# A two-block transformer on one core: router matmuls split into halves, expert gates moved into the first expert step, norms by halves, masks written singly, parameter loads moved

## The reference

```python
x = x + ((g_gla * y_gla + g_att * y_att) @ w_out[l])
x = x + hier_moe(rms_norm(x, norm2_g[l]), ...)   # 32 experts: group by argmax, then the top 2 of its 8
...
for i in range(2):                               # second block
    z = rms_norm_2(h, g_mix[i]) @ w_in[i]
    h = h + concatenate([y_a, y_b, y_c]) @ w_out[i]
    hn = rms_norm_2(h, g_ffn[i])
    h = h + (swiglu(hn, ...) if i == 0 else moe_swiglu(hn, ...))   # 8 experts, top 2
    h = h + (p[i] @ ple_proj_w[i]) * sigmoid(rms_norm_2(h, g_ple[i]) @ ple_gate_w[i])
return rms_norm_2(h, g_final)
```

## Time and profile before

| | |
|---|---|
| median of 3 runs | 2471.05 us (2470.52 to 2474.22) |
| profiled execution | 2472.59 us, of which the span of the trace is 2470.8 us |
| PE busy | 2319.1 us, 94% |
| DVE busy | 1842.4 us, 75% |
| ACT busy | 1467.2 us, 59% |
| POOL busy | 49.6 us, 2% |
| granted TensorE clock, mean | 0.971 |

### The profile page before, as it was taken

The page is one execution under the profiler, slowest core; times in us unless marked ns, Lnnn a source line. Parts: engine busy times, 40 slices in busy tenths (PEclk is TensorE's granted clock), DMA queues, the critical chain, the costliest instruction groups (busy, mean ns, idle before and its releaser), DMA issues.

```text
span 2470.8 us, 30555 instructions
## 1 busy us (share of the span) xinstructions
PE 2319.1 (94%) x12418; PEld 1891.6 (77%) x12418; DVE 1842.4 (75%) x1894; ACT 1467.2 (59%) x1400; POOL 49.6 (2%) x47
## 2 busy tenths in 40 slices
PE   7999987999999997988999998879999999999996
PEld 6878766888888885776788777668888888888885
DVE  5885658888898985776554577578888978888884
ACT  5354536776777774534443553466776767767764
POOL 0000000000000000020000002000000000000000
PEclk9999998999999998999999999989999999999999
DMA  9444445999999997406464551249999989999990
GB/s 231 128 124 136 153 145 186 363 367 358 366 359 367 357 368 231 138 3 196 138 203 171 166 163 50 81 177 363 356 366 357 358 300 349 358 368 355 366 344 34
DMA packets 281227, 617.64 MB, mean 250 GB/s; under 512 B 31848, under 2 KB 130408, under 8 KB 243696
## 3 DMA queue, kind: packets, MB, share of 16 engines
q1 hardware_dynamic: 279664, 611.33, 71.4%
q10 hardware_dynamic: 1408, 4.19, 0.5%
HBM read 612.34 MB, written 1.05 MB: 248 GB/s over the span
## 4 chain that ended last, share of the span: by engine, by line
PE 86%; DVE 7%; ACT 4%; issue 2%; POOL 0%; DMA 0%; DVEq 0%; ACTq 0%; SPq 0%
PE ps L566 25%; PE ps L567 25%; PE ps L568 25%; DVE ring_parts L590 2%; PE ps L2745 2%; PE ps L2098 1%; ACT high_parts L586 1%; PE ps L3023 1%; PE ps L667 1%; DVE arena L3280 0%; DVE arena L1325 0%; PE ps L3036 0%; PE ps L2068 0%; PE ps L2109 0%; PE ps L2110 0%
## 5 line engine op out<-in xcount | busy, mean ns | idle before, releaser
L590 DVE TENSOR_TENSOR ring_parts<-ring,high_parts 128x2048 fp32r<-128x2048 f32 (+1 forms) x574 | 1283.4, 2276 | 181.6 <-ACT high_parts L586 170.0
L586 ACT CAST high_parts<-ring 128x2048 fp32r<-128x2048 f32 (+1 forms) x574 | 1079.5, 1897 | 203.9 <-PE ps L568 190.6
L568 PE MATMUL ps<-high_parts,arena_parts 128*128 128x512 f32 (+2 forms) x1560 | 620.2, 398 | 0.0
L566 PE MATMUL ps<-high_parts,hT_parts 128*128 128x512 f32 (+2 forms) x1120 | 456.4, 408 | 30.5 <-DVE ring_parts L590 12.6
L567 PE MATMUL ps<-ring_parts,hT_parts 128*128 128x512 f32 (+2 forms) x1120 | 445.3, 398 | 0.0
L566 PE MATMUL ps<-high_parts 128*128 128x512 f32 x912 | 365.2, 400 | 0.0
L567 PE MATMUL ps<-ring_parts,high_parts 128*128 128x512 f32 x912 | 359.3, 394 | 0.0
L568 PE MATMUL ps<-high_parts 128*128 128x512 f32 x912 | 356.5, 391 | 0.0
L568 PEld LDWEIGHTS ps<-high_parts,arena_parts 128*128 128x128 f32 x1560 | 299.5, 192 | 68.9
L566 PE MATMUL ps<-high_parts,arena_parts 128*128 128x512 f32 x744 | 293.8, 395 | 3.2 <-DVE arena_parts L2273 2.3
L567 PE MATMUL ps<-ring_parts,arena_parts 128*128 128x512 f32 x744 | 292.9, 394 | 0.0
(11 more groups left out here) (525 smaller groups left out, 1831.0 us busy)
## 6 DMA issues: line engine op xcount, KB each, us to landing
ring<-in_moe_w SPq DMA_DIRECT2D x248, 1024.0 KB, 5.4
ring<-in_w_gate SPq DMA_DIRECT2D x64, 1024.0 KB, 5.3
ring<-in_w_up SPq DMA_DIRECT2D x64, 1024.0 KB, 5.2
ring<-in_w_down SPq DMA_DIRECT2D x64, 1024.0 KB, 5.3
ring<-in_w_in SPq DMA_DIRECT2D x104, 256.0 KB, 4.5
ring<-in_ffn_w SPq DMA_DIRECT2D x44, 512.0 KB, 4.8
ring<-in_w_in SPq DMA_DIRECT2D x20, 1024.0 KB, 5.0
ring<-in_moe_w SPq DMA_DIRECT2D x32, 512.0 KB, 4.8
```

The costliest lines, as they stand in the source:

```text
L566: pe.matmul(dst, a_hi, b_hi, start=first, stop=False, skip_group_check=True)
L568: return pe.matmul(dst, a_lo, b_hi, start=False, stop=last, skip_group_check=True)
L586: act.copy(high_flat(p), raw_flat(p)).then_inc(upper, 1)
L590: dve.tensor_tensor(raw_flat(p, ring_parts_flat), raw_flat(p), f32(high_flat(p)), ALU.subtract).then_inc(split, 1)
```

## The change

- **Routers.** The router matmuls of half of x stand inside the last projection; x·gain is made in halves before rstd is known; ACT multiplies it by rstd into the high rows, DVE (not POOL) makes the low rows; the slots of the tokens come right behind "routed", and two barriers between the stages are gone.
- **Gates.** The gates are made on DVE and ACT behind the first four splits of the first expert step. PE's `gates(b)` stands behind the last up piece of a step, not behind up 1, and waits for a new signal; this holds in each bucket or group that has one, so in the second group of `moe2` too.
- **Norms.** One half of the squares is made with the first half of x, and the table of Sqrt (in the feed-forward that of Silu too) is asked for by a small instruction ahead of the need. DVE adds the halves.
- **Feed-forward.** The split of the first down piece is moved ahead of the stage.
- **Masks.** POOL signals each of the two masks by itself; the wait for a mask ends earlier; the last LT mask is left out; POOL's copy comes behind the first pair. DVE makes TT before T.
- **Low-rank slots.** 9 becomes 10, and 12 becomes 13.
- **Parameter loads.** For layer 0 they stand behind four pieces of `in_0`, not six, and wait for the transposes of x, not for the last expert's matmuls.

```diff
@@ out_1 (and out_1_2), PE and DVE
+                if slot == 2 * (n_ab + 15):
+                    router_half_pe(pe, moe1, 0)
...
+                    if slot == 7 and l:
+                        router_half_pe(pe, moe2, 0)
...
+                    moe_gained_dve(dve, moe1, 0)
...
+        def norm_half_act(act, half):
+            for t in range(NT):
+                cols = slice(half * 512, (half + 1) * 512)
+                ins = act.activation(nt_sq[:, t * 512:(t + 1) * 512], x[:, t, cols], ACT.Square, accum_out=half_sums[half][:, t:t + 1])
+            if half:
+                ins.then_inc(sig("norm_sq"), 1)
+            else:
+                astep(act, ins)
+                act.activation(spare_cell, ident[:, 0:1], ACT.Sqrt)
...
+        def split_low_dve(dve, f):
+            dve.wait_ge(sig("moe_xh"), f.number)
+            for t in range(NT):
+                ins = dve.scalar_tensor_tensor(out=m_xl[:, t, :], in0=nt_xn[:, t, :], scalar=rstd[:, t:t + 1], in1=f32(m_xh[:, t, :]),
+                                               op0=ALU.mult, op1=ALU.subtract)
+            ins.then_inc(sig("moe_xl"), 1)
...
+            split_low_dve(dve, moe1)
+            place_dve(dve, moe1)
+
+        def gates1_dve(dve):
...
@@ the expert step, PE, ACT, DVE
                 up(st, 1)
-                if grouped:
-                    gates(b)
                 for h in range(2, len(st.up)):
                     if h == 2 and held:
                         pe.wait_ge(sig("moe_hid"), held.no)
                     up(st, h)
+                if grouped:
+                    pe.wait_ge(*ended(f"{f.name}_gates"))
+                    gates(b)
...
+                if st is f.plan[0]:
+                    router_exp_act(act, f)
                 if grouped:
                     gate(b)
...
+                if st is f.plan[0]:
+                    gates1_dve(dve) if f is moe1 else gates2_dve(dve)
...
@@ RWKV, PE and POOL
-                elif slot == 9:
+                elif slot == 10:
...
-                    pe.wait_ge(*at("rw_lm", k))
+                    pe.wait_ge(*at("rw_lm", 2 * k - 1))
...
-                        pool.wait_ge(*at(f"rw_z_psum{k - 1}"))
-                    pool.tensor_tensor(w_Lm, w_L, wide(low_b[:, k, :], NB), ALU.mult)
-                    pool.tensor_tensor(w_LTm, w_LT, wide(up_b[:, k, :], NB), ALU.mult).then_inc(sig("rw_lm"), 1)
+                    pool.tensor_tensor(w_Lm, w_L, wide(low_b[:, k, :], NB), ALU.mult).then_inc(sig("rw_lm"), 1)
+                    if k + 1 < LEV:
+                        if k > 1:
+                            pool.wait_ge(*at(f"rw_z_psum{k - 1}"))
+                        pool.tensor_tensor(w_LTm, w_LT, wide(up_b[:, k, :], NB), ALU.mult).then_inc(sig("rw_lm"), 1)
...
@@ SP
-                    stream(sp, pieces[0:6])
-                    sp.wait_ge(used, moe1.until)
+                    stream(sp, pieces[0:4])
+                    sp.wait_ge(sig("xT_psum"), XT_AT["mix0"] + KC // 2)
                     load_layer(sp, 0)
-                    stream(sp, pieces[6:10])
+                    stream(sp, pieces[4:10])
```

More of the change, by code:

```diff
@@ L706, in xT_ready, with norm_whole_act @@
                 pe.wait_ge(sig("xT_lower"), XU_AT[name] + 2 * half + 2)
-        def norm_squares_act(act):
+        half_sums, spare_cell = [small[:, 108 + NT * h:108 + NT * h + NT] for h in range(2)], small[:, 104:105]
+        def norm_whole_act(act):
             for t in range(NT):
-                ins = act.activation(nt_sq, x[:, t, :], ACT.Square, accum_out=small[:, t:t + 1])
+                ins = act.activation(nt_sq, x[:, t, :], ACT.Square, accum_out=half_sums[0][:, t:t + 1])
                 if t + 1 < NT:
@@ L720, in norm_mean_dve @@
             dve.wait_ge(sig("norm_sq"), n + 1)
+            vstep(dve, dve.tensor_tensor(small[:, 0:2], half_sums[0], half_sums[1], ALU.add))
             dve.tensor_scalar(small[:, 2:4], small[:, 0:2], 1.0 / D, EPS, ALU.mult, ALU.add).then_inc(sig("norm_ms"), 1)
@@ L1469, in first_dve @@
             evac_half(dve, "dve", "n2", g2T, None, 1, (6, 7))
+            moe_gained_dve(dve, moe1, 1)
         def first_mix_pool(pool):
@@ L1518, in emit, with router_half_pe, router_pe @@
         assert MR.at <= MR_AT + MR_SIZE
[L1520 to L1526, removed]
+        def router_half_pe(pe, f, half):
+            w, n = (r1_w, 36) if f is moe1 else (r2_w, NE2)
+            xT_ready(pe, PLAIN[f.number - 1], half)
+            for t in range(NT):
+                for c in range(4 * half, 4 * half + 4):
+                    mm = pe.matmul(ps[:, 4 + t, 0:n], hT[:, c, t * P:(t + 1) * P], w[:, c, :], start=(c == 0), stop=(c == KC - 1),
+                                   skip_group_check=True)
+            if half:
+                mm.then_inc(sig("router_logits"), 1)
+        def router_pe(pe, f):
+            router_half_pe(pe, f, 1)
             pe.wait_ge(sig("routed"), f.number)
@@ L1593, in router_norm_dve, with router_norm_act @@
             dve.wait_ge(sig("rstd"), n + 1)
[L1595 to L1598, removed]
+        def router_norm_act(act, f):
+            n = NORMS.index(PLAIN[f.number - 1])
+            act.wait_ge(evac_dve, jobs_of["out_1" if f is moe1 else "out_1_2"][-1].evac)
+            norm_half_act(act, 1)
+            norm_root_act(act, n)
+            act.wait_ge(sig("rstd"), n + 1)
+            for t in range(NT):
+                act.wait_ge(sig("moe_xg"), 4 * f.number)
+                ins = act.mul(m_xh[:, t, :], nt_xn[:, t, :], rstd[:, t:t + 1])
+            ins.then_inc(sig("moe_xh"), 1)
         def router1_act(act):
-            router_norm_act(act, "n2", jobs_of["out_1"][-1])
-            moe_split_act(act, moe1)
+            router_norm_act(act, moe1)
             act.wait_ge(sig("router_group"), 1)
@@ L1800, in dense_act @@
                     held = (k, t)
-                    if k + 1 < f.steps:
+                    if k + t == 0:
+                        pass
+                    elif k + 1 < f.steps:
                         split_high(act, f.up[k + 1][t])
@@ L1823, in dense_dve @@
                 for t in range(NT):
[L1824 removed]
+                    if k and t == 0:
                         split_low(dve, f.down[k])
```

109 lines of the change are left out of this document (58 added, 51 removed).

## The result

The change makes the kernel slower by about a quarter of a per cent: 2478.33 us median (2471.17 to 2484.66, 20 runs) against 2472.23 us (2468.05 to 2476.95, 20 runs), ratio 1.0026, 95% interval [1.0017, 1.0035]. I had predicted 2470 and "no measurable change" as the likeliest; the time lies inside the range given (2459 to 2479), but at its upper end, and clear of no change on the slower side.

The account below looks back on a forecast made before the run. PE was taken as the bound, so only its stalls between stages count. Gains and losses (9.5 + 7.3 - 6.5 - 4.7 - 6.6 - 3.5 + 4.0 + 2.9 - 1.35) sum to +1.1 us: 2471.05 becomes 2470, range 2459 to 2479.

Parts of the forecast that it names:

- no measurable change: Whole kernel: time the same within 0.2%, 2466.1 to 2476.0 us, likeliest 2470; chance 0.40.
- What bounds the kernel: Mid-experts PE is fully busy at full clock; only the few PE stalls between stages count.
- Routers: Before both expert stages: selection matrix and first expert matmul come sooner, gains of 9.5 and 7.3 us.
- Gates, first steps and second group: Expert steps: chain behind the moved gates stands uncovered; loss 3.24 us in `moe1` and `moe2` each, 4.7 in `moe2`'s second group.
- Clock behind new stalls: Behind three new PE stalls: half-clock spells at 2.2 us each, loss 6.6 us, between 0 and 9.
- `in_0` and the parameter loads: Start of `in_0`: transposes sooner but shift later behind loads and six pieces; net -3.5 us, between +4 and -6.
- Masks: Levels 4 and 5: PE's first block starts 1.0 us sooner, twice per layer; gain 4.0 us for two layers.
- Low-rank slots, ple, `in_1`: Later low-rank slots: -0.25 us in layer 1; squares and table load ahead of evacuation in ple, `in_1`, last norm: -1.35 us.
- Feed-forward: Stall before the feed-forward: tables asked for ahead, up 1 casts behind silu; gain 2.9 us (2.0 to 3.7).
- The slower rival: `in_0`: transposes' issue time does not move, shift lands late, PE's slot 8 5 us late; 2477 us, chance 0.24.

Follow-up runs that it names:

- r1_router_whole: Changed kernel with the shift ahead of the last four `in_0` pieces, plus both router matmul halves at the router, none inside the projection: 2462.09 us, ratio 0.9952.
- b1_only_sp: Kernel before with only the parameter loads moved (four pieces, wait for the transposes, loads, six pieces): 2480.53 us, ratio 1.0033.
- a4_masks_old: Changed kernel with the masks as before (one signal for both, copy first, T before TT): 2483.54 us, ratio 1.0051, 5 runs.

## Why the prediction was wrong, by its steps

- **What bounds the kernel: right.** The experts' middle did not move; every microsecond is in a stall between stages, or in the clock behind it.
- **Routers: mechanism right, sizes a little high.** 9.1 and 6.0 us, not 9.5 and 7.3. The piece that I had wrong is the half inside the projection. I let rstd decide when the logits come; in fact the second half of the router matmuls did, which PE began 1.06 us late and at a falling clock (2.55 us for 16, not 1.83). r1_router_whole shows that moving the half early is a loss.
- **Gates, first steps and second group: right.** 3.24 and 4.7 predicted, 3.2, 3.1 and 4.8 in the trace.
- **Clock behind new stalls: right.** 2.3, 2.2 and 2.3 us where 2.2 was taken. The small matmuls in the stalls didn't keep it up.
- **`in_0` and the parameter loads: the step that failed.** I wrote "-3.5, between +4 and -6". Measured in the trace: +5.1 for the earlier transposes (I took 2.2, or 3.5 with DVE's part), and 15.2 lost from there to the low-rank matmuls, 10 us net, outside the bounds; b1_only_sp puts it at -7.5 by itself. The mechanism, the shift waiting behind six pieces, was the right one. Its size was wrong because I priced SP's issuing (15.7 us for six pieces) and then let the shift land as fast as before. I also read the earlier trace rows as if issuing had set the shift's time there; but SP was done with its pieces at 981.5 and issued the shift at 989.34, when z was ready and the DMA engines stood idle. In the changed kernel SP issued the six in 7.38 us, and the data came later: with slot 8 put at 1005.7, 41 us behind my transposes at 965, it came 47.5 us behind them. To this come the half clock behind a wait of 13.01 us (2.5 us) and the low-rank slot that had been moved one later. The gain on the other side was misread too: I took the last stage's 6.24 us for a wait without loads beside it, but without them this wait is 2.6 to 3.5 us. By the Trainium skill, "DMA: Bandwidth & Descriptors", section on queues, rings and completion order, which I had cited against the change, descriptors on a DMA engine are consumed in ring order. The runs agree: the shift has landed 6.1 us behind its issue with no piece in front, 16.6 us with six.
- **Masks: failed too, by 4.0 us.** The step "PE starts 1.0 us sooner, twice per layer" was right to the tenth for the start of the block, and worth nothing: what is late next is DVE's copy of that block's product, behind side work that I had not followed and that takes 1 us longer with POOL beside it. I had asked what PE waits for first in a level, not what ends the level.
- **Low-rank slots, ple, `in_1`: right within a microsecond, the masks apart.** The idle was only moved: 1.91 us at L2616 for the 1.86 us taken away.
- **Feed-forward: right**, 1.9 for 2.9 us.
- **Not foreseen:** PE's issue wait in the last stage, 6.24 us before, is 2.89 here, and between 2.56 and 6.58 in the runs above; nothing of the change touches it.

Terms of 4.0 (masks), 6.6 (the loads, -10.1 for -3.5), 1.7 (routers), 1.0 (feed-forward) and 0.7 us (small ones) too good, less the 3.0 us of the last stage, turn +1.1 into about -10; the traces say -12.1, of which 2.0 came before the first edited stage, and the medians -6.1. That the median still lies within the range was luck: two terms missed by more than the whole sum, and the last stage gave back nearly 3 us that nothing in the change explains. The slower rival had the late shift as its mechanism with 2477, a microsecond from the median, at a chance of 0.24. But it made that hang on transposes that don't move; they did move, and the shift came late all the same.

**Open.** The runs of the changed kernel spread over 13.5 us (2471.17 to 2484.66), those of before over 8.9. With one trace of it I can't say which stage varies in it. Across the traces of the variants three places differ with no edit of the variant there: the offset to before at 350 us (-0.3 to +3.0), the wait for slot 8 where the loads stand as in the change (10.7 to 13.0 us in four traces of such kernels), and the issue wait in the last stage (2.6 to 6.6). Nor is it settled why a4_masks_old is 5 us slower than the changed kernel.

## What to carry to other kernels

A DMA that another engine waits for must be priced with the bytes queued in front of it, not with the time its issuer needs to reach it: put the small one that is awaited first, and the bulk that is needed later behind it. When an instruction is moved out of a stall, follow the engine that it leaves and the one that it joins to the *next* wait before giving it a price; in-order side work there took the whole gain of the masks. And each new stall of PE here (3.02 with 2.24 us, 4.74, 13.01) cost 2.2 to 2.5 us again in clock, so small work is best left where it fills a wait.

## What the runs showed of the hardware

- Twenty small loads in flight at the end of `moe1` made PE restart later: 8.1 to 9.3 us with them (three traces), 2.6 to 3.5 us without (eleven traces). In the trace of before, no packet of the instruction queues starts on the DMA engines between 957.5 and 964.3, while they are busy with the loads. The same gap is 6.8 to 6.9 us in all three traces with the loads and at most 2.5 in the eleven without. So PE's restart goes with the instruction packets; that their fetch is what PE waits for is still argued, not shown.
- SP issued six 1 MB loads in 7.38 us but the data took longer than that, and the shift issued behind them landed 16.6 us later, against 6.1 with an idle queue: issue time was no measure of the transfer.
- Two waits of 3.02 and 2.24 us with a 1 us burst of PE between them bring a window at clock 0.50 as one long wait does; waits of 0.85 and 1.54 do not the earlier trace rows. A single short wait can go either way: in the trace of before, the clock stays up behind the 1.86 us at 1008.19 and falls for 3.4 us behind the same wait in layer 1 (1433.98).
- A DVE product of 128x128 numbers took 1.24 us beside a POOL operation of 1.44 us, and 0.29 us without one (L3282 and L3242 above).
